# The moving inputs of a float32r matmul stream, 64 bytes lower against the weight ring

## What is computed

```python
h = rmsnorm(x, norm_g)
v, bg, cg, za, u, zb, ga, gb = split(h @ w_in)                 # 2048 -> 14336
ya = (bg * causal_conv3(cg * v, conv_w) * silu(za)) @ w_out_a
yb = gelu(s5_scan(u, ...)); yb = yb * sigmoid(yb @ w_glu + b_glu)
yb = (yb * silu(zb)) @ w_out_b
x = rmsnorm(x + (sigmoid(ga) * ya + sigmoid(gb) * yb) @ w_o, final_g)

u = rms_norm(x, norm1_g)
q, k, v, z = split(u @ w_in_2)                                 # attention 3 x 1024, rwkv 3360
mixed = concat([dilated_attention(q, k, v, bias), rwkv7_time_mix(z, ...)])
h = x + mixed @ w_out_2
gate, up = split(rms_norm(h, norm2_g) @ w_gate_up)             # 2048 -> 2 x 5632
return rms_norm(h + (silu(gate) * up) @ w_down, final_g_2)
```

## Time and profile before

| | |
|---|---|
| median of 3 runs | 2267.27 us |
| the profiled execution's own time | 2267.02 us |
| its span, first to last instruction | 2265.3 us |
| mean granted TensorE clock | 0.993 |
| busy: PE / PEld / DVE / ACT / POOL | 98% / 96% / 69% / 46% / 12% |
| moved by DMA | 387.8 MB, 171 GB/s |

### The profile page before, as it was taken

The page is one execution under the profiler, slowest core; times in us unless marked ns, Lnnn a source line. Parts: engine busy times, 40 slices in busy tenths (PEclk is TensorE's granted clock), DMA queues, the critical chain, the costliest instruction groups (busy, mean ns, idle before and its releaser), DMA issues.

```text
span 2265.3 us, 51607 instructions
## 1 busy us (share of the span) xinstructions
PE 2219.6 (98%) x20556; PEld 2163.5 (96%) x20556; DVE 1568.1 (69%) x2060; ACT 1040.4 (46%) x1357; POOL 265.0 (12%) x178
## 2 busy tenths in 40 slices
PE   7999999999999999999999999899999999999997
PEld 7999999999999989999999788799999999999997
DVE  7799989889545667778766577676666666654444
ACT  6544444444544444566344344554444444443443
POOL 0344444444100000100011000000000000000000
PEclk9999999999999999999999899999999999999999
DMA  7555555555555555555555011255555555556553
GB/s 262 177 170 181 176 180 176 177 178 186 189 191 185 187 196 193 189 177 174 201 176 181 29 49 49 77 186 186 185 186 185 186 186 185 185 180 190 183 181 136
DMA packets 107104, 387.81 MB, mean 171 GB/s; under 512 B 12032, under 2 KB 12160, under 8 KB 106752
## 3 DMA queue, kind: packets, MB, share of 16 engines
q1 hardware_dynamic: 104400, 375.44, 50.8%
q0 software_dynamic: 2176, 9.78, 1.3%
q10 hardware_dynamic: 432, 1.21, 0.1%
HBM read 384.29 MB, written 2.10 MB: 171 GB/s over the span
## 4 chain that ended last, share of the span: by engine, by line
PE 92%; DVE 4%; ACT 2%; issue 1%; DMA 0%; DVEq 0%; SPq 0%; ACTq 0%
PE ps_main L1691 28%; PE ps_main L1693 27%; PE ps_main L1692 27%; PE ps_aux L1919 2%; DVE w_lo L977 1%; PE ps_main L1919 1%; PE ps_main L1990 1%; ACT w_hi L495 1%; PE ps_aux L1940 1%; DMA w_raw<-wmain 0%; PE ps_main L1992 0%; PE ps_main L1991 0%; PE ps_aux L1760 0%; PE ps_aux L1748 0%; PE ps_main L1964 0%
## 5 line engine op out<-in xcount | busy, mean ns | idle before, releaser
L977 DVE TENSOR_TENSOR w_lo<-w_raw,w_hi 128x1024 fp32r<-128x1024 f32 x718 | 918.3, 1295 | 459.1 <-ACT w_hi L495 453.8
L495 ACT ACTIVATE w_hi<-w_raw 128x1024 fp32r<-128x1024 f32 x718 | 747.4, 1046 | 739.6 <-PE ps_main L1693 729.6
L1691 PE MATMUL ps_main<-xs,w_hi 128*128 128x256 f32 x1664 | 467.8, 281 | 2.7 <-DVE w_lo L977 1.8
L1692 PE MATMUL ps_main<-xs,w_hi 128*128 128x256 f32 x1664 | 464.5, 279 | 0.0
L1693 PE MATMUL ps_main<-xs,w_lo 128*128 128x256 f32 x1664 | 464.2, 279 | 0.0
L1691 PE MATMUL ps_main<-x3s,w_hi 128*128 128x256 f32 x1408 | 394.4, 280 | 0.0
L1693 PE MATMUL ps_main<-x3s,w_lo 128*128 128x256 f32 x1408 | 392.8, 279 | 0.0
L1692 PE MATMUL ps_main<-x3s,w_hi 128*128 128x256 f32 x1408 | 392.8, 279 | 0.0
L1691 PEld LDWEIGHTS ps_main<-xs,w_hi 128*128 128x128 f32 x1664 | 312.4, 188 | 9.5 <-DVE w_lo L977 5.0
L1693 PEld LDWEIGHTS ps_main<-xs,w_lo 128*128 128x128 f32 x1664 | 312.6, 188 | 0.0
L1692 PEld LDWEIGHTS ps_main<-xs,w_hi 128*128 128x128 f32 x1664 | 311.4, 187 | 0.0
(11 more groups left out here) (420 smaller groups left out, 3777.1 us busy)
## 6 DMA issues: line engine op xcount, KB each, us to landing
w_raw<-wmain SPq DMA_DIRECT2D x622, 512.0 KB, 3.4
w_raw<-wdown SPq DMA_DIRECT2D x80, 512.0 KB, 3.7
w_raw<-wdown SPq DMA_DIRECT2D x16, 256.0 KB, 2.7
bias<-bias POOLq DMA_DIRECT2D x8, 384.0 KB, 3.4
x_res<-xt POOLq DMA_DIRECT2D x4, 512.0 KB, 6.5
out<-x_res SPq DMA_DIRECT2D x3, 512.0 KB, 2.8
x_first<-xt SPq DMA_DIRECT2D x2, 512.0 KB, 7.1
x_first<-xt ACTq DMA_DIRECT2D x2, 512.0 KB, 9.4
```

The lines of the kernel that those rows point to most:

```text
L495: nc.scalar.activation(whi[:, s, 0:width], raw[:, s, 0:width], ACT.Copy).then_inc(hi_ready, 1)
L977: V.tensor_tensor(wlo[:, s, 0:width], raw[:, s, 0:width], whi[:, s, 0:width].bitcast(F32), ALU.subtract)\
L1691: nc.tensor.matmul(out, whi[:, s, w], high[:, k, :], start=(first and kk == 0), stop=False)
L1692: nc.tensor.matmul(out, whi[:, s, w], low[:, k, :], start=False, stop=False)
```

## The change

The start of everything that `wk` makes moves from 320 to 256 bytes past a multiple of 1024. To make the room, gg (64 bytes) goes into the gap between `par` and `const`, and phi and rho take its place. No other line differs, and the instructions of all engines stand in the same order as before.

```diff
-        gg = at("gg", small + 14 * K, [KB])
-        phi = at("phi", small + 14 * K + 64, [STATE_TILES])
-        rho = at("rho", small + 14 * K + 192, [STATE_TILES])
-        work = small + 14 * K + 320
+        gg = at("gg", 64 * K + 1344, [KB])
+        phi = at("phi", small + 14 * K, [STATE_TILES])
+        rho = at("rho", small + 14 * K + 128, [STATE_TILES])
+        work = small + 14 * K + 256
```

## The result

The changed kernel takes 2299.0 us (median of 4, 2297.92 to 2304.37) against 2265.5 for the kernel before: the ratio is 1.0164, 95% interval [1.0145, 1.0182]. It is **slower by 1.6%**, 33.5 us. The forecast was 2201 us with a range up to 2292.

What follows compares the result with a forecast made beforehand. TensorE's 17,040 matmuls at 117.8 ns spacing were taken to bound the kernel. From 2267.0 us, 71 came off for 113.3 ns spacing, 3 and 2 were added for convolution and recurrence: 2201 us, range 2190 to 2292.

Steps and rivals of the forecast that it cites:

- What bounds the kernel: Whole kernel: TensorE busy 98%; time is 17,040 matmuls of 256 columns times their spacing of 117.8 ns, plus a little.
- The quantum: Matmul stream: the rhythms differ by 6 ns at the start, about 16 columns (64 bytes); a 64-byte shift is that step.
- the two rhythms: Same tiles' matmuls start 117.8 ns apart mostly, 113.3 ns in part of rkv and qkv; either keeps going until interrupted.
- I take the lower end: Spacing after the change: of bounds from 71 us less to 13 or 80 us more, 113.3 ns nearly everywhere was chosen.
- (b): Stage u, x_raw_l at 0 against the ring: matmuls alternate; same place modulo 1024 costs 10 ns, half a period away nothing.
- The upper bound from the u stage's mixture: Stage u: 118.6 ns spacing, 0.8 ns over 117.8; for 15,900 matmuls 13 us more.
- The mild rival: Even slices' input comes nearer the weights and pays as in the u stage's mixture: 13 us more, 2280 us; chance 0.13.
- The rival "slower": Even slices pay as inputs come 64 bytes nearer the weights: 2280 us mild (0.13), some 2347 full (0.09).
- the loss of the fast rhythm: In rkv and qkv, 760 matmuls at 113.3 ns falling back by 4.45 ns each: only 3 us more.
- The rival "faster than the 113.3": All moved streams: excess nearly gone, 109.2 ns spacing, 137 us less with some 12 given back: 2142 us; chance 0.10.
- The waits of the convolution stage: Convolution: at the new pace VectorE would be 94% busy; 3 us charged for new short waits.
- the sum: Whole kernel: profiled 2267.0 us - 71 for spacing + 3 for convolution waits + 2 for attention and recurrence = 2201 us; chance 0.28.

Runs made afterwards that it cites:

- off0: The changed kernel with its input tiles at 0 past a multiple of 1024, as the ring, instead of 256: 2298.4 us beside 2261.2 of the kernel before.

## Why the prediction was wrong

- **What bounds the kernel** held: TensorE's spacing, 17,040 of them, and nothing else changed. So did the coverage of all other edits (tables: same time).
- **The quantum** held in part: I wrote that 16 columns, 64 bytes, part the two rhythms and that a shift by 64 bytes is a shift by that step. All rhythms are whole numbers of such steps over their repeat. But a tile moved by 64 bytes didn't change the spacing by one step: from 320 to 256 each matmul became a third of a step longer (17.67 to 18).
- **The step that failed is "I take the lower end"**, and under it the reading of (b), "the same place modulo 1024 costs 10 ns, half a period away costs nothing extra". From one tile whose class differs from its partner's I made a curve over distance, dearer toward 0, on which 256 is better than 192. At distance 0 for all inputs there is no such price of one slice against the next (off0). The evidence against the curve stood in my text, 192 and 320 equally dear, and was given less weight than the tile. What the runs showed in its place: 120.0 ns at 256, the dearest spacing of all runs, and the same 120.0 at 0.
- **Period and neighbours.** In the runs the distance counts modulo 256: 0 and 256 give 108 steps; 64, 320 and 832 give 106 with some 102; 192, 448 and 704 give 102 and 106 mixed; 384, alone in its class, gives 106.8. 256 is in the dearest class, and my steps had no row of it but x_raw_l's, whose short matmuls (0.12 us) I read as cheap.
- **The term's size**: 15,900 x (-4.45 ns) was forecast, 15,900 x (+2.2 ns) came. The upper bound from the u stage's mixture (118.6 ns) was no bound either. Of three matmuls there only the one of x_raw_l, at 0 and 512, was in the class into which the change moved all three, and I took the mixture's excess, 0.8 ns, as the price of all. Nor is 0.8 exact: 230 is a count of whole matmuls, and the starts in stage u are 713.3 ns apart over six, 118.9 each, 1.1 ns over. The mild rival's 13 us were therefore too few, and the range that rested on it, to 2292, missed 2299.
- **The rival "slower"** had the side and not the mechanism: it asked for longer matmuls on even slices, and all became 120.0 alike, without a lengthening of every second slice. Its limit (above 353 ns for three) was passed: 360. For the loss of the fast rhythm it had 3 us; it was 5, as the new spacing is 120.
- **The rule** that TensorE's two read ports are independent and that PE never waits on anyone (the Trainium skill, SBUF — State Buffer, Who interferes with whom) would leave placement without effect, as I wrote. These runs disagree: the same instructions took 2200 to 2299 us, as tiles moved. That the two reads wait for each other is a possible cause, but no run shows such a wait itself.
- **The rival "faster than the 113.3"** came nowhere: no placement holds fewer than 102 steps.
- **The clock** made 6 us between the two profiled executions, and no term had that. It is luck of the execution: at like clocks the change cost some 38 us, not 33.5.
- The pace of 113.3 ns that I forecast exists, but for w_hi at 192 and w_lo at 64, and there 2204.0 us were measured where the sum has 2201. That this is within 3 us is partly luck, since the sum started from an execution at the low clock, 6 us over most others. The waits of the convolution stage I had at 3 us; PE's idle time before line 1691's matmuls with xs (zb, convolution and gb) went from 2.7 us to 7.5:

```profile
L1691 PE MATMUL ps_main<-xs,w_hi 128*128 128x256 f32 x1664 | 462.3, 278 | 7.5 <-DVE w_lo L977 6.7
```

What stays open: why 192 with 64 holds the fast rhythm and 64 with 192 doesn't, and what at a stretch's start draws one or the other. A model of the reads that gives all these counts I don't have. Beside the pair 192 and 64, moving x_raw_l to its partner's place, so that stage u might hold 102 as well, wasn't tried.

## What to carry to other kernels

Where matmuls with 256 float32r columns run back to back, each with its own weights, read the spacing of starts and compare it with columns by clock; an excess of several per cent, with no idle time, may be the placement of the moving tile against the stationary one, in steps of 64 bytes. It can't be reasoned from one odd tile: run the classes modulo 256 and the pairs, each costs one run, and count steps in the trace, which tells more than the time. Time the winner in several executions, since in some placements two rhythms are possible and executions of one kernel differ in them; and compare the granted clocks before a difference of a few us is put down to a change.

## What the runs showed of the hardware that I had not expected

- Such a stream runs in rhythms that repeat exactly, over a whole number of steps of 16 columns (6.67 ns at the full clock): 17 or 18 steps for one matmul, 53 for three, 107 for six, 210 for 12, 266 and 267 for 15, 426 for 24, each held for hundreds of us, where the columns alone are 16 for each. At the granted clock of 1.2 GHz, in the one stretch read the earlier trace rows, there was no excess.
- The relation is one of the moving tile to the weights: 64 bytes more on both left the 106 steps (91%), on the ring alone 108 steps became 102 and 106.
- One program had executions of 2210 and 2257 us (the ring alone moved), at mean granted clocks of 0.998 and 0.992: 0.006 x 2257 = 14 us at most are the clock's. That the rest of the 47 us is rhythm was seen in the two traces at 192, and only argued for these ten.
- Weights of the two halves in different classes don't in general give the mean of the classes (the pair 64, 192 has 107, over both), and the pair 192, 64 holds the 102 nearly throughout, which no single distance did.
